# One-column sums, compressed scores and AdaLN turns as matmuls of 32 weight columns each

## What is computed

```python
def rmsnorm(x, g):
    y = xf * lax.rsqrt(jnp.mean(xf * xf, axis=-1, keepdims=True) + EPS)
    return (y * g.astype(jnp.float32)).astype(x.dtype)

# AdaLN: nine vectors of 1024 per layer, for the tokens (c) and for the context (c_ctx)
m = (sc @ ada_w[i] + ada_b[i]).reshape(-1, N_MOD, D_MODEL)[:, :, None, :]
x = x + 0.5 * m[:, 2] * swiglu(rmsnorm(x, norm_g[i, 0]) * (1 + m[:, 1]) + m[:, 0], wg, wu, wd)

# second block, per layer
o_h = rmsnorm_2(o_h, hgrn_out_norm[layer]).reshape(B, S, HGRN_WIDTH) * jax.nn.silu(hz)
s_c = jnp.einsum('btghd,bngd->bghtn', qblk, k_cmp) * scale      # 15 compressed keys
p_c = masked_softmax(s_c, cmp_end[None, :] <= t[:, None], -1)
```

## Time and profile before

| | us |
|---|---|
| median of 3 runs | 2177.68 |
| lowest, highest | 2177.62, 2182.33 |
| the profiled execution | 2182.2 |
| its span | 2180.5 |
| TensorE matmul busy | 2059.2 |
| VectorE busy | 1421.3 |
| ScalarE busy | 966.6 |
| GpSimd busy | 229.8 |

### The profile page before, as it was taken

The page is one execution under the profiler, slowest core; times in us unless marked ns, Lnnn a source line. Parts: engine busy times, 40 slices in busy tenths (PEclk is TensorE's granted clock), DMA queues, the critical chain, the costliest instruction groups (busy, mean ns, idle before and its releaser), DMA issues.

```text
span 2180.5 us, 40888 instructions
## 1 busy us (share of the span) xinstructions
PE 2059.2 (94%) x17519; PEld 1948.4 (89%) x17519; DVE 1421.3 (65%) x1707; ACT 966.6 (44%) x1093; POOL 229.8 (11%) x195
## 2 busy tenths in 40 slices
PE   5899999999998999999999999999999988999997
PEld 4899999987765999999999999999999868999976
DVE  3546777779778966777754554456765645776553
ACT  2433443343332654333543443446545624745541
POOL 1000000010003201000000000001430001341000
PEclk9999999999998979999999999999989988999988
DMA  9778868853232426888655435545543414544410
GB/s 328 239 271 269 277 222 291 288 178 102 80 95 80 172 91 227 294 293 292 213 178 188 159 122 187 191 156 175 157 136 117 155 40 125 171 132 141 135 55 20
DMA packets 270802, 384.01 MB, mean 176 GB/s; under 512 B 8441, under 2 KB 230727, under 8 KB 270679
## 3 DMA queue, kind: packets, MB, share of 16 engines
q1 hardware_dynamic: 246983, 293.59, 41.9%
q0 software_dynamic: 22288, 85.02, 11.1%
q10 hardware_dynamic: 1408, 3.59, 0.4%
HBM read 381.06 MB, written 1.11 MB: 175 GB/s over the span
## 4 chain that ended last, share of the span: by engine, by line
PE 80%; DVE 12%; ACT 3%; issue 3%; DMA 1%; SPq 0%; DVEq 0%; ACTq 0%
PE bank L696 22%; PE bank L698 22%; PE bank L697 22%; DVE w_hl L1877 2%; ACT w_hl L1423 1%; PE bank L726 1%; DVE conv_acc L2207 1%; PE bank L761 1%; PE bank L746 1%; PE bank L1207 1%; PE bank L773 1%; DVE e_long L2258 1%; PE bank L1180 1%; DVE ada_acc L1950 1%; DVE scratch L1911 1%
## 5 line engine op out<-in xcount | busy, mean ns | idle before, releaser
L1877 DVE TENSOR_TENSOR w_hl<-raw,w_hl 128x2048 fp32r<-128x2048 f32 (+1 forms) x281 | 654.3, 2329 | 389.9 <-ACT w_hl L1423 389.6
L1423 ACT ACTIVATE w_hl<-raw 128x2048 fp32r<-128x2048 f32 (+1 forms) x281 | 532.3, 1894 | 218.6 <-PE bank L698 215.3
L696 PE MATMUL bank<-u_hl,w_hl 128*128 128x256 f32 x2080 | 593.4, 285 | 1.6 <-issue 1.6
L698 PE MATMUL bank<-u_hl,w_hl 128*128 128x256 f32 x2080 | 588.2, 283 | 1.2 <-issue 1.2
L697 PE MATMUL bank<-u_hl,w_hl 128*128 128x256 f32 x2080 | 588.3, 283 | 0.0
L696 PEld LDWEIGHTS bank<-u_hl,w_hl 128*128 128x128 f32 x2080 | 396.2, 190 | 13.6 <-issue 9.8
L697 PEld LDWEIGHTS bank<-u_hl,w_hl 128*128 128x128 f32 x2080 | 396.4, 191 | 0.0
L698 PEld LDWEIGHTS bank<-u_hl,w_hl 128*128 128x128 f32 x2080 | 395.9, 190 | 0.0
L696 PE MATMUL bank<-h_hi,w_hl 128*128 128x256 f32 x800 | 226.9, 284 | 4.0 <-DVE h_lo L1974 4.0
L697 PE MATMUL bank<-h_lo,w_hl 128*128 128x256 f32 x800 | 226.0, 283 | 0.0
L698 PE MATMUL bank<-h_hi,w_hl 128*128 128x256 f32 x800 | 226.0, 282 | 0.0
(11 more groups left out here) (413 smaller groups left out, 3970.9 us busy)
## 6 DMA issues: line engine op xcount, KB each, us to landing
ada<-in_ada_w POOLq DMA_DIRECT2D x72, 1024.0 KB, 6.7
raw<-in_w_in SPq DMA_DIRECT2D x60, 1024.0 KB, 5.2
raw<-in_ffn_w_gate SPq DMA_DIRECT2D x55, 1024.0 KB, 7.2
raw<-in_ffn_w_up SPq DMA_DIRECT2D x55, 1024.0 KB, 5.4
raw<-in_ffn_w_down SPq DMA_DIRECT2D x55, 1024.0 KB, 5.1
raw<-in_ssd_w_in SPq DMA_DIRECT2D x20, 1024.0 KB, 5.3
raw<-in_w_out SPq DMA_DIRECT2D x16, 1024.0 KB, 5.1
raw<-in_ssd_w_out SPq DMA_DIRECT2D x8, 1024.0 KB, 5.2
```

Of the source, the lines that this page charges most:

```text
L696: pe.matmul(out_, wh, xh, start=start, stop=False, skip_group_check=True)
L698: return pe.matmul(out_, wl, xh, start=False, stop=stop, skip_group_check=True)
L1423: nc.scalar.activation(whi[slot][:, 0:n], raw[slot][:, 0:n], ACT.Copy).then_inc(S["hi_done"], 1)
L1877: ve.tensor_tensor(wlo[slot][:, 0:n], raw[slot][:, 0:n], whi[slot][:, 0:n].bitcast(F32), ALU.subtract)\
```

## The change

A helper `by_strips` issues one matmul as four, each with 32 of the 128 weight columns and writing the 32 partitions of the bank that belong to them. It replaces the single matmul in `norm_by_token`, in `ada_turn_one`, in the HGRN output norm and in the compressed scores. The mask matmul of the scores and the spreading matmuls stay whole. In the pairs of `ffn` the AdaLN turn moves from between the two blocks of the up chunk to behind it. In the last pair it stays where it was.

```diff
+            def by_strips(bk, c0, c1, lhs, rhs, start, stop):
+
+                for s0 in range(0, P, 32):
+                    m = pe.matmul(bank[bk][s0:s0 + 32, c0:c1], lhs[:, s0:s0 + 32], rhs, start=start, stop=stop,
+                                  skip_group_check=True)
+                return m
@@ norm_by_token
                     for tile in range(TT):
-                        dst = b[:, 2 * tile:2 * tile + 2] if fold else b[:, tile:tile + 1]
-                        m = pe.matmul(dst, scratch[:, k, tile * P:(tile + 1) * P],
+                        c0, c1 = (2 * tile, 2 * tile + 2) if fold else (tile, tile + 1)
+                        m = by_strips(bk, c0, c1, scratch[:, k, tile * P:(tile + 1) * P],
                                       fold_cols[:, k, :] if fold else ones[:, 0:1],
-                                      start=at == 0 and tile == 0, stop=k == KB - 1, skip_group_check=True)
+                                      at == 0 and tile == 0, k == KB - 1)
@@ ada_turn_one
                 for blk in range(4):
-                    m = pe.matmul(bank[3][:, blk:blk + 1], ada_acc[:, blk * P:(blk + 1) * P], ones[:, 0:1],
-                                  start=True, stop=True)
+                    m = by_strips(3, blk, blk + 1, ada_acc[:, blk * P:(blk + 1) * P], ones[:, 0:1], True, True)
@@ ffn, pair
                     pe.wait_ge(S["mult_done"], pairs + j)
-                    hidden(g + 4, 1, None, j - 1, turn_one if ada_too == "one" else None)
+                    hidden(g + 4, 1, None, j - 1)
+                    if ada_too == "one":
+                        turn_one()
@@ HGRN output norm
-                            m = pe.matmul(bank[7][:, un:un + 1], scratch[:, h, tile * P:(tile + 1) * P], ones[:, 0:1],
-                                          start=True, stop=True)
+                            m = by_strips(7, un, un + 1, scratch[:, h, tile * P:(tile + 1) * P], ones[:, 0:1], True, True)
@@ compressed scores
                     for h in range(H2):
-                        m = pe.matmul(bank[0][:, tile * P + 16 * h:tile * P + 16 * h + 16],
-                                      nq[:, h, tile * P:(tile + 1) * P], kcmp[:, h // 4, :], start=False, stop=True,
-                                      skip_group_check=True)
+                        m = by_strips(0, tile * P + 16 * h, tile * P + 16 * h + 16, nq[:, h, tile * P:(tile + 1) * P],
+                                      kcmp[:, h // 4, :], False, True)
```

More of the change, by code:

```diff
@@ L714, in norm_by_token @@
                 n, b = N[name], bank[BY_TOKEN[name]]
+                bk = BY_TOKEN[name]
                 fold = name == "pre0"
```

## The result

The changed kernel takes 2157.39 us, the median of 4 runs (2156.38 to 2160.57), against 2180.01 us of the kernel before beside it: a ratio of 0.9896, 95% interval 0.9878 to 0.9914. That is 22.6 us less.

A forecast was written before the change was run, and what follows sets the result against it. TensorE was taken as the bound, busy 2059.2 of 2180.5 us. Savings of 8.3 + 5.6 + 4.3 + 3.5 + 4 = 25.7 us gave a median of 2152, likeliest 2147 to 2155, range 2146 to 2164.

The forecast's parts named there:

- (b): Rival: loop branch behind the AdaLN turns not covered, 20 x 0.1 to 0.3 us, so 2154 to 2158; chance 0.12.
- Strip pace: All four groups: strips follow each other 8.7 ns apart, four taking 35 ns against 112 for one full record.
- third rival: Strips with one streamed column go at 27 ns, not 8.7; 5.8 us slower, 2183; chance 0.05.
- AdaLN turns: Feed-forward: 26 turns, each 0.80 us in strips for 1.14, taken as 0.32 saved each, 8.3 us.
- by that it is just covered, 0: Loop branch behind the moved turn: strips worth 0.5 to 0.6 us against 0.5 needed, so no cost.
- VectorE behind the moved turn: Chunk's end: VectorE's next product starts some 0.8 us later, made good within the pair, 2.8 us of cover left.
- Norms: Nine norms: roots start earlier, 0.58 us in each of six, 2.1 in pre1, 0 in post0 and post1; 5.6 us.
- HGRN norm: Output norm in two layers: 1.65 us in strips for 3.81, 2.16 saved in each, 4.3 us.
- Scores: Compressed scores, twice per layer: 0.98 us in strips for 1.81, 0.83 saved four times, taken as 3.5 us.
- Clock: Half-clock stretches behind long rows of narrow full matmuls: 7.7 us if four go, taken as 4, bounds -3 and 8.
- Rival (a): Clock does not get better, since falls come elsewhere: 21.7 us saved, 2156; chance 0.20.
- (d): Rival: VectorE's chain in the attention stage swallows the HGRN and scores gains, no clock gain; 2164; chance 0.08.

The follow-up runs named there:

- e1_mid: The changed kernel with the AdaLN turns, still in strips, put back between the two blocks of the up chunk; 2152.4 us, ratio 0.9876.
- e1_whole_moved: The kernel before with only the AdaLN turns, as whole matmuls, moved to the end of the up chunk; 2176.3 us, ratio 0.9982.
- e3_after: The changed kernel itself, unaltered, timed once more on another chip; 2155.4 us, ratio 0.9891.
- e2_hgrn4: e1_mid with the strips of the HGRN output norm issued four times in a row, same sums each time; 2179.2 us, one run.
- e1_steps: The changed kernel with the turn 3, 6, 9 and 15 matmuls before the up chunk's end, by feed-forward; 2149.5 us, ratio 0.9868.

## Why the prediction was right, point by point

The time, 2152 forecast and 2157.4 measured, lies in the range of 2146 to 2164, but outside the 2147 to 2155 that had the largest chance; it fell in case (b), 2154 to 2158. It came about by terms that were off in both directions.

- **Strip pace.** Right. 32 records in 0.26 us, 64 in 0.56; from record to record it is 8.5 to 9.1 ns with 1 and with 2 streamed columns and 8.8 with 16. The third rival (27 ns, 2183 us) and the rule of the Trainium skill ("TensorE: Matmul & The Clock Gate", section "Wait — 56ns, not 53.3ns?") that start to start never falls below about 25 ns do not hold for strips side by side; the trace disagrees with it.
- **AdaLN turns, 8.3 us.** The step that failed is "by that it is just covered, 0". The pair gives 0.33 us in the middle (`e1_mid`), as worked out. But the branch costs 0.3 us in each of 17 turns and 0.1 in three more, at a loop's end: 5.4 us, which leaves 3.3. The prediction had named the place, the mechanism and the price ("up to 0.3 us in each of 20 turns, 6 us") and taken the wrong end, by a margin of 0.1 us: it took the 0.2 us of the way into the strips for cover, but 16 instructions of lead, which were 1.9 us of whole matmuls, are only 0.14 us of strips. At 885.7 it ran the branch while the strips, which end at 885.78, had less than 0.1 us left, and PE had its next matmul at 886.19.
- **VectorE behind the moved turn.** Right: it waited 1.33 us for the strips and the product came 0.45 us after the sum, and no pair grew by it (`e1_whole_moved`).
- **Norms, 5.6 us.** 5.7 measured from last square to root, with post0 and post1 at 0 and pre1 at 2.0. At `pre0` the 0.7 us were lost to the stop of 2 us.
- **HGRN norm, 4.3 us.** 4.5: each layer moved up by 2.23 us at the first matmul behind it; the row with both steps takes 1.6 us for 3.81.
- **Scores, 3.5 us.** 3.9: 0.94 and 0.99 a tile for 0.83, since the way out to the mask is shorter than taken.
- **Stops for code.** Not in the prediction at all: a term at nothing, without a reason. 2.8 us in before, some 7 in the changed kernel: -4.6 us in the profiled execution, and 2 us less of them in `e3_after`. The prediction read only what an engine waits for, and did not ask whether short instructions can be had as fast as they run.
- **Clock, 4 us, bounds -3 and 8.** Probably too small: the mean went from 0.9519 to 0.9584, which by the line above is 8.6 us (3.5 with the slope within the changed kernel, 10.0 with that of before). The falls behind the HGRN norm are gone as said. Right behind the scores the clock now stays at 1.00 too, but 6.8 us at half clock come 15 us later (1729.9); other falls went that were not in the sum. Why before has the lowest clock of all, even below `e1_whole_moved` with the same work (0.955), is not settled, and so how much of these 8.6 us the strips earned is not shown, beyond the two falls behind the HGRN norm.
- **Rival (a)** did not come, **(d)** neither: DVE's chain moved along.

The sum of what was found is 3.3 + 5.7 + 4.5 + 3.9 - 4.6 + 8.6 = 21.4 us for 22.6 in the medians; with the other two slopes it is 16.3 and 22.8. By this sum the clock gave 4.6 us more than forecast and the stops took 4.6 away, which cancelled by luck; what remains is the branch, 5.0 us less at the turns, against 0.7 us more at the other three parts. The number was better than its parts.

## What to carry to other kernels

In this kernel the records of float32 matmuls with 128 weight columns and 1 streamed column stood 0.10 to 0.11 us apart, nearly as far as those of `mm3` with 256 (0.12); four strips of 32 columns did the work of one in a third of that. With the ways in and out a turn of 4 matmuls went from 1.13 to 0.79 us, a row of 16 from 3.81 to 1.60. Short instructions use up two reserves that long ones hide. Keep three full matmuls between such a block and a loop's branch (three were enough here, none was not), and look on the page for waits for "issue" of 1 to 3 us in straight code behind strips. Before an edit is credited with 2 or 3 us, count those stops and the granted clock in both traces: the mere length of the code moves the stops, and two kernels with the same work differed in their clock (0.952 and 0.955).

## What the runs showed of the hardware that was not expected

- PE's code is fetched in packets of 16 KB (1.75 MB in 107), one for 128 matmul records in straight code. Strips back to back go through one in 1.1 us at full clock, and the next landed 3.5 and 5.5 us after the one before (`e2_hgrn4`); PE goes on 1.2 to 1.7 us after the landing.
- Three whole matmuls of 0.12 us behind a strip block hid the branch of a loop (`e1_steps`); with none the pair was 0.3 us longer.
- The span follows the mean granted clock: in 41 executions of before by 1.55 us for each 0.001, which is 91% of their spread, but in 16 of the changed kernel by 0.55, 28% of it.
- The clock fell to half while PE was busy without a gap, right behind, once within, the 3.5 us row of 32 records with 128 weight columns and 1 streamed column, in both layers of four kernels; behind the same sums once in strips it never did (nine executions).
